# Placing the modulation's column sums in the wait of the norm behind the MLP, and multiplying the first two input panels together

## The chip, the cores and the metric

The kernel runs on 1 core of one Trainium2 chip, in one launch. The metric is the device time in microseconds (us) from the first to the last instruction with what lies around them; lower is better. The core has five engines that run in parallel, each through its own instructions in order: TensorE (PE, matrix products into PSUM, eight banks of 128x512 float32), VectorE (DVE), ScalarE (ACT), GpSimd (POOL) and SyncE (SP, which only issues DMAs here). They wait for each other on semaphores.

## The reference

Two transformer-like blocks over x of 512 tokens by 1024 features, all float32. The first is an RWKV-7 branch and a short convolution, gated and merged, then cross attention to a memory, then an MLP. The second is a gated window attention and a spatial gating unit under an adaptive norm. The change lies at the seam of the two:

```python
# end of the first block
hm = rms_norm(x, norm_mlp)
x = x + jnp.square(jax.nn.relu(hm @ w_up)) @ w_down        # w_up 1024x4096, w_down 4096x1024
x = rms_norm(x, norm_final)
# start of the second block
ada = silu(c) @ w_ada + b_ada                              # c: 1024, w_ada: 1024x3072
shift, scale, gate = jnp.split(ada, 3)
h = _rms(x, g_pre) * (1.0 + scale) + shift
proj = h @ w_in                                            # split into q, k, v, z_a, u_b, v_b, z_b, gate logits
...
x = x + gate * _rms(y, g_post)                             # the last line; x is the residual
```

## The kernel before, in words

**Layout.** Activations lie feature-major: a tile is 128 features by 512 tokens, and a tensor of 1024 features is 8 tiles (KT = 8). xT is the residual. Every large product is cut into panels of 128 output features. A panel's weights, 128x1024 float32, come in one DMA of 512 KB on SP's queue into one of three slots (w_raw, W = 3); ACT rounds them to w_hi, DVE writes the rest w_raw - w_hi to w_lo, and the operand is split into opX_hi and opX_lo the same way. A panel is then 8 steps of 3 matmuls (w_hi by hi, w_hi by lo, w_lo by hi), 24 matmuls of 128x512, summed into bank 0 or bank 1 by turns.

**What sets the order.** The order is written out by hand. SEGMENTS names 210 panels in sequence: ..., up3 (8 panels), down3 (8), qkv (7), ub (4), vb (4), za, zb, gates2 and so on. Each engine has a program that walks the same sequence with the class Panels: begin(i) waits on PE for the panel's w_lo and for its bank to be emptied, step(i, k) is one of the 8 steps (on ACT and DVE the steps K_HIGH = 5 and K_LOW = 6 make w_hi and w_lo of panel i + 2), and end(i) is what ACT, DVE or POOL do with the result. multiply() issues begin and all steps of one panel without its end, leave() the end, to(name) whole panels up to a segment. What stands between these calls is placed there by hand. SP waits for panel i - 3 to be multiplied before it issues panel i's DMA into the same slot.

**The seam.** ada_sum holds silu(c) times w_ada, summed over the 8 row tiles by DVE during down0 and down1: 128 partial sums for each of 3072 columns. Summing these over the partitions needs PE: 24 matmuls ("columns"), each with 128 columns of ada_sum as weights and one column of a constant as the moving operand (L361, out 128x1). In float32 each shows as two records in the profile, so 48. Before, all 24 stand between up3 and down3 and write bank 6; DVE then makes adac (24 columns: shift, scale, gate), gain2, gain3 and gate2 in four small instructions. During down3 ACT squares each new residual tile twice (plain, and times norm_final) and POOL adds the squares to acc and acc2. Behind down3's last panel, two norms follow each other without a tile-wide step between: PE sums acc over the partitions (token_sums, 4 columns, 8 records, into bank 7) and acc2 (bank 6), DVE and ACT form 1/rms as a column, DVE widens it (token_wide), and PE turns it into a row over tokens (token_spread, 4 transposes of 128x128, into bank 5). Then DVE and ACT make opA_hi and opA_lo of the 8 tiles in turn: scale(k) on DVE, the high part on ACT, the low part on DVE. The first panel of qkv starts with tile 0 and waits at each step (operand_low).

**Behind the first panel.** During qkv's first panel DVE widens the first norm's column (r1c to r1, rstd_first), PE spreads it into bank 6 behind that panel, and DVE scales the residual in eight instructions: xT times norm_final times bank 6. These stand on DVE ahead of the copy that empties bank 1 of the first panel. The scaled residual is read only at the very end (last_add).

Of the kernel before, what the change touches and what calls it, by code (L numbers as in the profile page):

```python
# [10 lines left out]
D = 1024  # L11
# [108 lines left out]
class Panels:  # L120
# [18 lines left out]
    def leave(self):  # L139
        self.end(self.i)  # L140
        self.i, self.k = self.i + 1, 0

    def to(self, name):
# [5 lines left out]
def build(nc, x_in, mem_in, panels, ada_w, vec_in, mat_in, win_in, lora_in, pos_in, sink_in, ws_in,  # L149
# [111 lines left out]
    def mat(name):  # L261
        a, w = MAT[name]
        return mats[:, a:a + w]
# [33 lines left out]
    def left_after(i):  # L297
# [49 lines left out]
        sem("angle_step"), sem("sine"), sem("rotated"), sem("rope_cosine"), sem("rope_sine"), sem("rope_made"))  # L347
    silu_half = sem("silu_sigmoid")

# [7 lines left out]
    def tensor_program():  # L357
        pe = nc.tensor

        def mm(o, lhsT, rhs, start=True, stop=True):  # L360
            return pe.matmul(o, lhsT, rhs, start=start, stop=stop, skip_group_check=True)  # L361
# [307 lines left out]
        p.leave()  # L669
        p.to("down3")  # L670
        pe.wait_ge(ada_step, KT)
        for c in range(24):
            ins = mm(bank[6][:, c:c + 1], ada_sum[:, c * NP:(c + 1) * NP], mat("mean")[:, 0:1])
        ins.then_inc(ada_mm, 1)
        p.to("qkv")
        pe.wait_ge(summed, 2 + 3 * KT)
        token_sums(acc, bank[7])
        pe.wait_ge(summed2, KT)
        token_sums(acc2, bank[6])
        token_spread(rstd, bank[5], 1)  # L680
        p.multiply()
        token_spread(r1, bank[6], 2)
        p.leave()
        p.to("za")
# [406 lines left out]
    def gpsimd_program():  # L1091
# [145 lines left out]
        gp.memset(acc[:, :], 0.0).then_inc(cleared, 1)  # L1237
        p.to(None)
        for n, k in enumerate((0, 2, 4)):
            gp.wait_ge(sv_step, 12 + k + 1)  # L1240
            tt(xT[:, k, :], xT[:, k, :], P[:, k, :], ALU.add).then_inc(last_add, 1)

    def vector_program():
        ve = nc.vector

        def tt(o, a, b, op):
            return ve.tensor_tensor(o, a, b, op)  # L1247
# [39 lines left out]
        def end(i):  # L1287
# [61 lines left out]
            elif name[:4] == "down":  # L1349
                tt(xT[:, m, :], ps, xT[:, m, :], ALU.add).then_inc(left[j], 1)  # L1350
            elif name == "qkv":
                ve.tensor_copy(P[:, m, :], ps).then_inc(left[j], 1)
            elif name in ("za", "zb"):
                ve.wait_ge(silu_half, (0 if name == "za" else 4) + m + 1)
                tt(P[:, (ZA if name == "za" else ZB) + m, :], ps, tmp[j][:, :], ALU.mult).then_inc(left[j], 1)
            elif name == "out2":
                ve.wait_ge(squared, 5 * KT + m + 1)
                ts(P[:, m, :], ps, gate2[:, m:m + 1], ALU.mult).then_inc(left[j], 1)
# [196 lines left out]
        for h in range(XH):  # L1555
# [13 lines left out]
        p.leave()  # L1569
        p.to("down3")  # L1570
        ve.wait_ge(ada_mm, 1)
        stt(adac, bank[6][:, 0:24], float(D), vecs[:, COL["b_ada"]:COL["b_ada"] + 24], ALU.mult,
            ALU.add).then_inc(ada_cols, 1)
        ve.wait_ge(ada_cols, 1)
        stt(gain2, adac[:, 8:16], 1.0, vecs[:, COL["g_pre"]:COL["g_pre"] + 8], ALU.add, ALU.mult).then_inc(ada_cols, 1)
        ve.wait_ge(ada_cols, 2)
        tt(gain3, gain2, vecs[:, COL["norm_final"]:COL["norm_final"] + 8], ALU.mult).then_inc(ada_cols, 1)
        tt(gate2, adac[:, 16:24], vecs[:, COL["g_post"]:COL["g_post"] + 8], ALU.mult).then_inc(ada_cols, 1)
        p.to("qkv")

# [14 lines left out]
        token_reciprocal(head_cols, 1)  # L1595
        token_wide(rc, rstd)
        ve.wait_ge(tok_spread, 1)
        ve.wait_ge(ada_cols, 4)
# [9 lines left out]
        for k in range(KT):  # L1608
# [3 lines left out]
            if k + 2 < KT:  # L1612
                scale(k + 2)
        p.multiply()
        token_wide(r1c, r1)
        ve.wait_ge(tok_spread, 2)
        for k in range(KT):
            stt(xT[:, k, :], xT[:, k, :], vec("norm_final", k), bank[6][:, :], ALU.mult, ALU.mult)
        p.leave()
        p.to("ub")  # L1620
# [227 lines left out]
```

## Time and profile before

| what | value |
|---|---|
| time, median of 3 runs | 1542.4 us (1537.39 to 1544.82) |
| the profiled execution's own time | 1547.85 us |
| its span, first to last instruction | 1546.5 us |
| mean granted TensorE clock | 0.97 of full |
| PE busy | 1454.3 us, 94% of the span |
| DVE, ACT, POOL busy | 788.1, 484.9, 171.2 us |
| HBM read | 130.86 MB, 86 GB/s over the span |

The profiled execution took 1.35 us more than its span; that is launch and end. It is 5.45 us above the median and above all three timed runs, so differences are worked out inside the trace and then taken from the median. PE waits for little; its clock is granted at one of two levels, shown as 1.00 (2.4 GHz) or 0.50 (1.2 GHz). A window's value between the two is a mix. Matmuls overlap, so the distance between two starts is what one costs, not its length: 128x512 shows 0.40 us of length at full clock and starts every 0.23 us.

### The profile page before, as it was taken

The numbers are of one execution on the slowest core, as the hardware profiler recorded it, in microseconds if no ns is written. First come the engines' busy times: TensorE is split into PE (matmuls) and PEld (weight loads), VectorE is DVE, ScalarE is ACT, GpSimd is POOL, SyncE is SP. The second block draws the span as 40 slices with busy tenths as digits, with TensorE's granted clock in tenths as the row PEclk, the third lists the DMA queues.
The fourth block names the chain that finished last, engine by engine and source line by source line (L and its number), as shares of the span: only waits on it lengthen the run. The fifth ranks groups of instructions, "written<-read, shape, count | busy, mean of one in ns | idle before, by whom it ended". The sixth has DMA issues, their size and how long they took to land.

```text
span 1546.5 us, 21133 instructions
## 1 busy us (share of the span) xinstructions
PE 1454.3 (94%) x9170; PEld 1138.3 (74%) x9170; DVE 788.1 (51%) x1069; ACT 484.9 (31%) x716; POOL 171.2 (11%) x155
## 2 busy tenths in 40 slices
PE   4999999999998999998999999999989999998995
PEld 3677686877766878876877787888867777777784
DVE  5364363645538654534464655535345344565544
ACT  4321222314134343224431222212232332663331
POOL 1120110202011220000200000000130011003122
PEclk9999899999998999999999999999889999999997
DMA  4110111112014224420244434322222223221221
GB/s 152 60 56 29 41 43 42 56 43 69 29 59 146 96 82 151 134 71 15 95 169 171 167 105 163 96 95 94 70 68 73 91 83 99 77 69 55 95 93 72
DMA packets 37579, 134.34 MB, mean 87 GB/s; under 512 B 4045, under 2 KB 5709, under 8 KB 36462
## 3 DMA queue, kind: packets, MB, share of 16 engines
q1 hardware_dynamic: 31392, 112.21, 21.7%
q0 software_dynamic: 1440, 13.63, 2.4%
q10 hardware_dynamic: 4654, 7.13, 1.4%
q8 instruction: 73, 1.20, 0.3%
q14 instruction: 20, 0.16, 0.0%
HBM read 130.86 MB, written 2.10 MB: 86 GB/s over the span
## 4 chain that ended last, share of the span: by engine, by line
PE 37%; issue 14%; DVE 6%; DMA 3%; ACT 3%; POOL 1%; POOLq 0%; DVEq 0%
PE bank L361 36%; DMA w_raw<-panels 3%; DVE w_lo L1247 1%; ACT w_hi L773 1%; POOL acc L1095 1%; PE bank L364 1%; ACT scores L773 1%; ACT L773 0%; DVE ada_sum L1255 0%; DVE xT L1247 0%; DVE tmp L1255 0%; DVE P L1247 0%; DVE tmp L1247 0%; ACT exp L773 0%; DVE xT L1255 0%
## 5 line engine op out<-in xcount | busy, mean ns | idle before, releaser
L361 PE MATMUL bank<-opA_hi,w_hi 128*128 128x512 f32 x1104 | 466.1, 422 | 39.2 <-DVE opA_lo L1255 18.3
L1247 DVE TENSOR_TENSOR w_lo<-w_raw,w_hi 128x1024 fp32r<-128x1024 f32 x210 | 261.4, 1246 | 387.7 <-ACT w_hi L773 387.7
L361 PE MATMUL bank<-opA_lo,w_hi 128*128 128x512 f32 x1104 | 443.0, 401 | 0.0
L361 PE MATMUL bank<-opA_hi,w_lo 128*128 128x512 f32 x1104 | 442.5, 401 | 0.0
L773 ACT ACTIVATE w_hi<-w_raw 128x1024 fp32r<-128x1024 f32 x210 | 221.8, 1057 | 433.3 <-DMA w_raw<-panels 430.9
L361 PEld LDWEIGHTS bank<-opA_hi,w_hi 128*128 128x128 f32 x1104 | 211.3, 191 | 105.1 <-issue 41.6
L361 PEld LDWEIGHTS bank<-opA_hi,w_lo 128*128 128x128 f32 x1104 | 211.7, 192 | 51.8
L361 PEld LDWEIGHTS bank<-opA_lo,w_hi 128*128 128x128 f32 x1104 | 212.2, 192 | 45.3 <-issue 2.7
L361 PE MATMUL bank<-opB_hi,w_hi 128*128 128x512 f32 x448 | 180.0, 402 | 6.9 <-DVE xT L1247 4.3
L361 PE MATMUL bank<-opB_lo,w_hi 128*128 128x512 f32 x448 | 178.4, 398 | 0.0
L361 PE MATMUL bank<-opB_hi,w_lo 128*128 128x512 f32 x448 | 178.4, 398 | 0.0
L361 PEld LDWEIGHTS bank<-opB_hi,w_hi 128*128 128x128 f32 x448 | 85.1, 190 | 29.5 <-issue 5.8
L361 PEld LDWEIGHTS bank<-opB_hi,w_lo 128*128 128x128 f32 x448 | 85.0, 190 | 20.8
L361 PEld LDWEIGHTS bank<-opB_lo,w_hi 128*128 128x128 f32 x448 | 85.2, 190 | 20.5 <-issue 0.2
L1095 POOL TENSOR_TENSOR acc<-acc,sq 128x512 f32<-128x512 f32 x32 | 43.0, 1344 | 374.3 <-issue 266.8
L773 ACT ACTIVATE opB_hi<-tmp 128x512 fp32r<-128x512 f32 x44 | 27.8, 632 | 106.8 <-DVE tmp L1255 62.9
L773 ACT ACT_TABLE_LOAD x40 | 51.3, 1283 | 6.4 <-DMA w_raw<-panels 5.7
L361 PE MATMUL bank<-mem_hi,w_hi 128*128 128x256 f32 x128 | 36.7, 287 | 3.3 <-DVE kvT L1247 3.3
L1247 DVE TENSOR_TENSOR xT<-bank,xT 128x512 f32<-128x512 f32 x48 | 32.9, 685 | 9.7 <-PE bank L361 9.7
L361 PE MATMUL bank<-mem_lo,w_hi 128*128 128x256 f32 x128 | 36.2, 283 | 0.0
L361 PE MATMUL bank<-mem_hi,w_lo 128*128 128x256 f32 x128 | 36.2, 282 | 0.0
L773 ACT ACTIVATE UV<-bank 64x64 f32<-64x64 f32 (+1 forms) x40 | 11.6, 291 | 72.0 <-PE bank L361 72.0
(272 smaller groups left out, 1451.2 us busy)
## 6 DMA issues: line engine op xcount, KB each, us to landing
w_raw<-panels SPq DMA_DIRECT2D x210, 512.0 KB, 3.5
ada_w<-ada POOLq DMA_DIRECT2D x8, 1536.0 KB, 7.6
xT<-x ACTq DMA_DIRECT2D x1, 2048.0 KB, 11.2
out<-xT SPq DMA_DIRECT2D x8, 256.0 KB, 2.1
xT<-x POOLq DMA_DIRECT2D x2, 512.0 KB, 10.0
xT<-x ACTq DMA_DIRECT2D x2, 512.0 KB, 12.1
memT<-mem ACTq DMA_DIRECT2D x1, 1024.0 KB, 13.5
mats<-mat ACTq DMA_DIRECT2D x1, 672.0 KB, 7.6
```

What stands on the lines that cost most here:

```text
L361: return pe.matmul(o, lhsT, rhs, start=start, stop=stop, skip_group_check=True)
L364: return pe.transpose(o, i, mat("ident"))
L773: return ac.activation(o, i, f, **kw)
L1095: return gp.tensor_tensor(o, a, b, op)
L1247: return ve.tensor_tensor(o, a, b, op)
```

## The change

The 24 column matmuls leave their place between up3 and down3. They are issued in three groups of 8 in the wait behind down3: part 1 (scale) into bank 3 ahead of the token sums, part 0 (shift) into bank 2 behind them and ahead of the spread, part 2 (gate) into bank 4 behind the spread. DVE's small instructions follow them, in groups of the same order. The first two panels of qkv are multiplied by the new method pair(), which issues step k of the one (bank 1) and step k of the other (bank 0) before step k + 1. The spread of the first norm's row moves behind both. DVE's eight instructions on the residual move to the four ends of the ub panels, two each, and POOL waits for all eight (x3_made) ahead of its last additions.

```diff
--- before.py
+++ after.py
@@ -139,6 +139,15 @@
     def leave(self):
         self.end(self.i)
         self.i, self.k = self.i + 1, 0
+
+    def pair(self):
+        self.begin(self.i)
+        self.begin(self.i + 1)
+        for k in range(KT):
+            self.step(self.i, k)
+            self.step(self.i + 1, k)
+        self.leave()
+        self.leave()
 
     def to(self, name):
         assert self.k == 0
@@ -345,7 +354,7 @@
         sem("token_spread"), sem("x4_scaled"))
     angle_step, trig_done, rot_mm, rope_pool, rope_sin, rope_done = (
         sem("angle_step"), sem("sine"), sem("rotated"), sem("rope_cosine"), sem("rope_sine"), sem("rope_made"))
-    silu_half = sem("silu_sigmoid")
+    silu_half, x3_made = sem("silu_sigmoid"), sem("x3_made")
 
     assert N_PANELS == panels.shape[0], (N_PANELS, panels.shape)
     sink_done, bn_step, ws_mm, ws_done, vn_v, vn_g, uz_done, sv_mm, sv_step = (
@@ -667,20 +676,24 @@
         pe.wait_ge(summed, 2 + 2 * KT)
         mean(acc, S)
         p.leave()
-        p.to("down3")
+        p.to("qkv")
+
+        def ada_columns(part):
+            for c in range(KT * part, KT * (part + 1)):
+                ins = mm(bank[2 + part][:, c:c + 1], ada_sum[:, c * NP:(c + 1) * NP], mat("mean")[:, 0:1])
+            ins.then_inc(ada_mm, 1)
+
         pe.wait_ge(ada_step, KT)
-        for c in range(24):
-            ins = mm(bank[6][:, c:c + 1], ada_sum[:, c * NP:(c + 1) * NP], mat("mean")[:, 0:1])
-        ins.then_inc(ada_mm, 1)
-        p.to("qkv")
+        ada_columns(1)
         pe.wait_ge(summed, 2 + 3 * KT)
         token_sums(acc, bank[7])
         pe.wait_ge(summed2, KT)
         token_sums(acc2, bank[6])
+        ada_columns(0)
         token_spread(rstd, bank[5], 1)
-        p.multiply()
+        ada_columns(2)
+        p.pair()
         token_spread(r1, bank[6], 2)
-        p.leave()
         p.to("za")
 
         def rotate(n, t):
@@ -1236,6 +1249,7 @@
         gp.wait_ge(weigh_mm, 2 * XH + 4)
         gp.memset(acc[:, :], 0.0).then_inc(cleared, 1)
         p.to(None)
+        gp.wait_ge(x3_made, KT)
         for n, k in enumerate((0, 2, 4)):
             gp.wait_ge(sv_step, 12 + k + 1)
             tt(xT[:, k, :], xT[:, k, :], P[:, k, :], ALU.add).then_inc(last_add, 1)
@@ -1350,6 +1364,10 @@
                 tt(xT[:, m, :], ps, xT[:, m, :], ALU.add).then_inc(left[j], 1)
             elif name == "qkv":
                 ve.tensor_copy(P[:, m, :], ps).then_inc(left[j], 1)
+            elif name == "ub":
+                ve.wait_ge(tok_spread, 2)
+                for k in range(2 * m, 2 * m + 2):
+                    stt(xT[:, k, :], xT[:, k, :], vec("norm_final", k), bank[6][:, :], ALU.mult, ALU.mult).then_inc(x3_made, 1)
             elif name in ("za", "zb"):
                 ve.wait_ge(silu_half, (0 if name == "za" else 4) + m + 1)
                 tt(P[:, (ZA if name == "za" else ZB) + m, :], ps, tmp[j][:, :], ALU.mult).then_inc(left[j], 1)
@@ -1567,16 +1585,19 @@
         p.multiply()
         inv_root(rstd[:, :], bank[7][:, :], 4)
         p.leave()
-        p.to("down3")
-        ve.wait_ge(ada_mm, 1)
-        stt(adac, bank[6][:, 0:24], float(D), vecs[:, COL["b_ada"]:COL["b_ada"] + 24], ALU.mult,
-            ALU.add).then_inc(ada_cols, 1)
+        p.to("qkv")
+
+        def ada_columns(part, n):
+            c = slice(KT * part, KT * (part + 1))
+            ve.wait_ge(ada_mm, n)
+            stt(adac[:, c], bank[2 + part][:, c], float(D), vecs[:, COL["b_ada"] + KT * part:COL["b_ada"] + KT * (part + 1)],
+                ALU.mult, ALU.add).then_inc(ada_cols, 1)
+
+        ada_columns(1, 1)
         ve.wait_ge(ada_cols, 1)
         stt(gain2, adac[:, 8:16], 1.0, vecs[:, COL["g_pre"]:COL["g_pre"] + 8], ALU.add, ALU.mult).then_inc(ada_cols, 1)
         ve.wait_ge(ada_cols, 2)
         tt(gain3, gain2, vecs[:, COL["norm_final"]:COL["norm_final"] + 8], ALU.mult).then_inc(ada_cols, 1)
-        tt(gate2, adac[:, 16:24], vecs[:, COL["g_post"]:COL["g_post"] + 8], ALU.mult).then_inc(ada_cols, 1)
-        p.to("qkv")
 
         def token_reciprocal(v, n):
             ve.wait_ge(tok_root, n)
@@ -1594,6 +1615,7 @@
         stt(rc, r1c, EPS, bank[6][:, 0:4], ALU.mult, ALU.add).then_inc(tok_var, 1)
         token_reciprocal(head_cols, 1)
         token_wide(rc, rstd)
+        ada_columns(0, 2)
         ve.wait_ge(tok_spread, 1)
         ve.wait_ge(ada_cols, 4)
 
@@ -1611,12 +1633,10 @@
                 ALU.subtract).then_inc(op_lo, 1)
             if k + 2 < KT:
                 scale(k + 2)
-        p.multiply()
+        ada_columns(2, 3)
+        ve.wait_ge(ada_cols, 5)
+        tt(gate2, adac[:, 16:24], vecs[:, COL["g_post"]:COL["g_post"] + 8], ALU.mult).then_inc(ada_cols, 1)
         token_wide(r1c, r1)
-        ve.wait_ge(tok_spread, 2)
-        for k in range(KT):
-            stt(xT[:, k, :], xT[:, k, :], vec("norm_final", k), bank[6][:, :], ALU.mult, ALU.mult)
-        p.leave()
         p.to("ub")
 
         TURN, MAGIC = 2 * np.pi, 1.5 * 2 ** 23
```

ACT's and SP's instructions stand in the same order before and after. Three places show the rest. In all of them opA and opB are the operands, w_hi2 is slot 2 of the high weights, and the number behind an underscore is a buffer's own. Line numbers of the change are 9 to 23 higher than before for the same helper.

The first place is PE behind the last matmul of down3, before:

```order
L361 MATMUL bank0<-opB_hi_52,w_lo1_58 128x512
L361 MATMUL bank7<-mats_74,acc_71 128x1 [waits squares_summed]
L361 MATMUL bank7<-mats_74,acc_71 128x1 x3
L361 MATMUL bank6<-mats_74,acc2_72 128x1 [waits squares2_summed]
L361 MATMUL bank6<-mats_74,acc2_72 128x1 x3
L364 MATMUL bank5<-mats_74,rstd_64 128x128 [waits token_wide]
L364 MATMUL bank5<-mats_74,rstd_64 128x128 x3
```

and in the change:

```order
L370 MATMUL bank0<-opB_hi_52,w_lo1_58 128x512
L370 MATMUL bank3<-mats_74,ada_sum_127 128x1 [waits ada_step]
L370 MATMUL bank3<-mats_74,ada_sum_127 128x1 x7
L370 MATMUL bank7<-mats_74,acc_71 128x1 [waits squares_summed]
L370 MATMUL bank7<-mats_74,acc_71 128x1 x3
L370 MATMUL bank6<-mats_74,acc2_72 128x1 [waits squares2_summed]
L370 MATMUL bank6<-mats_74,acc2_72 128x1 x3
L370 MATMUL bank2<-mats_74,ada_sum_127 128x1 x8
L373 MATMUL bank5<-mats_74,rstd_64 128x128 [waits token_wide]
L373 MATMUL bank5<-mats_74,rstd_64 128x128 x3
L370 MATMUL bank4<-mats_74,ada_sum_127 128x1 x8
```

acc and acc2 are the sums of squares, rstd the widened column of the norm. The three groups of ada_sum matmuls now stand ahead of the token sums, between these and the spread, and behind the spread; the 24 that stood between up3 and down3 are gone from there.

The second place is PE at the end of qkv's first panel and the start of the second, before:

```order
L361 MATMUL bank1<-opA_hi_50,w_hi2_62 128x512 [waits operand_low]
L361 MATMUL bank1<-opA_lo_51,w_hi2_62 128x512
L361 MATMUL bank1<-opA_hi_50,w_lo2_59 128x512
L364 MATMUL bank6<-mats_74,rstd_first_73 128x128 [waits token_wide]
L364 MATMUL bank6<-mats_74,rstd_first_73 128x128 x3
L361 MATMUL bank0<-opA_hi_50,w_hi0_60 128x512 [waits bank0_left,panel_low_made]
L361 MATMUL bank0<-opA_lo_51,w_hi0_60 128x512
L361 MATMUL bank0<-opA_hi_50,w_lo0_57 128x512
```

and in the change, PE from the first step of the pair:

```order
L370 MATMUL bank1<-opA_hi_50,w_hi2_62 128x512 [waits bank0_left,panel_low_made,operand_low,bank1_left]
L370 MATMUL bank1<-opA_lo_51,w_hi2_62 128x512
L370 MATMUL bank1<-opA_hi_50,w_lo2_59 128x512
L370 MATMUL bank0<-opA_hi_50,w_hi0_60 128x512
L370 MATMUL bank0<-opA_lo_51,w_hi0_60 128x512
L370 MATMUL bank0<-opA_hi_50,w_lo0_57 128x512
L370 MATMUL bank1<-opA_hi_50,w_hi2_62 128x512 [waits operand_low]
```

and PE from the end of its last step:

```order
L370 MATMUL bank0<-opA_lo_51,w_hi0_60 128x512
L370 MATMUL bank0<-opA_hi_50,w_lo0_57 128x512
L373 MATMUL bank6<-mats_74,rstd_first_73 128x128 [waits token_wide]
L373 MATMUL bank6<-mats_74,rstd_first_73 128x128 x3
L370 MATMUL bank1<-opA_hi_50,w_hi1_61 128x512 [waits bank1_left,panel_low_made]
```

Bank 1 and slot 2 belong to the first panel of qkv, bank 0 and slot 0 to the second, slot 1 to the third. Six matmuls stand behind each wait for an operand tile where three stood, and the four transposes of rstd_first stand ahead of the third panel where they stood ahead of the second.

The third place is DVE from the last operand tile on, before:

```order
L1255 SCALAR_TENSOR_TENSOR opA_lo_51<-tmp1_68,cols_76,opA_hi_50 128x512 [waits operand_high]
L1247 TENSOR_TENSOR w_lo1_58<-w_raw1_55,w_hi1_61 128x1024 [waits panel_high_made]
L1587 COPY rstd_first_73<-cols_76 128x512
L1255 SCALAR_TENSOR_TENSOR xT_49<-xT_49,vecs_75,bank6 128x512 [waits token_spread]
L1255 SCALAR_TENSOR_TENSOR xT_49<-xT_49,vecs_75,bank6 128x512 x7
L1352 COPY P_63<-bank1 128x512 [waits panel_multiplied]
L1247 TENSOR_TENSOR w_lo2_59<-w_raw2_56,w_hi2_62 128x1024 [waits panel_high_made]
L1352 COPY P_63<-bank0 128x512 [waits panel_multiplied]
```

and in the change:

```order
L1269 SCALAR_TENSOR_TENSOR opA_lo_51<-tmp1_68,cols_76,opA_hi_50 128x512 [waits operand_high]
L1269 SCALAR_TENSOR_TENSOR cols_76<-bank4,vecs_75 128x8 [waits ada_multiplied]
L1261 TENSOR_TENSOR cols_76<-cols_76,vecs_75 128x8 [waits ada_columns]
L1608 COPY rstd_first_73<-cols_76 128x512
L1261 TENSOR_TENSOR w_lo1_58<-w_raw1_55,w_hi1_61 128x1024 [waits panel_high_made]
L1366 COPY P_63<-bank1 128x512 [waits panel_multiplied]
L1261 TENSOR_TENSOR w_lo2_59<-w_raw2_56,w_hi2_62 128x1024 [waits panel_high_made]
L1366 COPY P_63<-bank0 128x512 [waits panel_multiplied]
```

Further on in the change, DVE at the ends of the first two ub panels:

```order
L1266 TENSOR_SCALAR sq1_70<-sq1_70 128x512 [waits angle_step]
L1265 TENSOR_SCALAR sq1_70<-sq1_70 128x512 [waits angle_step]
L1269 SCALAR_TENSOR_TENSOR xT_49<-xT_49,vecs_75,bank6 128x512 [waits token_spread]
L1269 SCALAR_TENSOR_TENSOR xT_49<-xT_49,vecs_75,bank6 128x512
L1261 TENSOR_TENSOR w_lo0_57<-w_raw0_54,w_hi0_60 128x1024 [waits panel_high_made]
L1269 SCALAR_TENSOR_TENSOR xT_49<-xT_49,vecs_75,bank6 128x512 [waits token_spread]
```

cols holds adac and the gains, P the results of qkv, sq the sine's argument. The eight instructions on xT stood ahead of the copy that empties bank 1; now two small ones stand ahead of w_lo1, and the residual is scaled by twos ahead of each w_lo in ub. The w_lo2 of qkv's fourth panel stands between the copies of the first two panels in both.

## Rows read from the trace of the kernel before

**Rows 1.** the profile page, part 1: busy time and share of the span.
```profile
PE 1454.3 (94%) x9170; PEld 1138.3 (74%) x9170; DVE 788.1 (51%) x1069; ACT 484.9 (31%) x716; POOL 171.2 (11%) x155
```

**Rows 2.** windows over every engine, from up3 to the norm; columns in the first row.
```profile
core 0: us, PE busy (x) PEld busy (x) DVE busy (x) ACT busy (x) POOL busy (x), PEclk, DMA share, GB/s
1090.76:1091.76 1.00, 1.00 (x11) 1.00 (x9) 0.96 (x3) 0.03 (x1) 0.00 (x0) 1.00 0.00 0
1094.20:1095.20 1.00, 1.00 (x6) 1.00 (x6) 0.00 (x0) 0.77 (x1) 0.00 (x0) 0.50 0.00 0
1103.47:1145.87 42.40, 42.40 (x182) 33.81 (x180) 12.83 (x14) 16.15 (x21) 17.83 (x14) 1.00 0.26 87
1151.00:1153.50 2.50, 1.12 (x4) 0.72 (x4) 0.94 (x5) 0.21 (x1) 0.00 (x0) 0.52 0.00 0
```

**Rows 3.** timeline of PE, up3 to down3: start, length, engine, line, operation [idle before it].
```profile
1090.76 8.12 PE L361 MATMUL bank<-mats,ada_sum 128*128 128x1 f32 x48
1098.74 0.77 PE L361 MATMUL bank<-opB_hi,w_hi 128*128 128x512 f32 x1
...
1103.47 0.40 PE L361 MATMUL bank<-opB_hi,w_lo 128*128 128x512 f32 x1
```

**Rows 4.** timeline of all engines, the wait of the norm behind down3.
```profile
1145.90 0.69 DVE L1247 TENSOR_TENSOR xT<-bank,xT 128x512 f32<-128x512 f32 x1
...
1148.56 1.26 POOL L1095 TENSOR_TENSOR acc<-acc,tmp 128x512 f32<-128x512 f32 x1
...
1149.87 1.05 PE L361 MATMUL bank<-mats,acc 128*128 128x1 f32 x8 [0.17 <-POOL acc L1095]
...
1152.31 1.12 PE L364 MATMUL bank<-mats,rstd 128*128 128x128 f32 x4 [1.39 <-DVE rstd L1587]
...
1155.00 0.75 DVE L1255 SCALAR_TENSOR_TENSOR opA_lo<-tmp,cols,opA_hi 128x512 fp32r<-128x512 f32 x1
...
1155.90 0.76 PE L361 MATMUL bank<-opA_hi,w_hi 128*128 128x512 f32 x1 [2.47 <-DVE opA_lo L1255]
```

**Rows 5.** timeline of PE, the first two panels of qkv and the start of the third.
```profile
1161.17 0.48 PE L361 MATMUL bank<-opA_hi,w_lo 128*128 128x512 f32 x1
...
1167.13 0.66 PE L364 MATMUL bank<-mats,rstd_first 128*128 128x128 f32 x4 [0.80 <-DVE rstd_first L1587]
1167.54 0.48 PE L361 MATMUL bank<-opA_hi,w_hi 128*128 128x512 f32 x1
...
1173.93 0.47 PE L361 MATMUL bank<-opA_hi,w_hi 128*128 128x512 f32 x1 [0.55 <-DVE P L1352]
```

**Rows 6.** timeline of DVE, the same stretch.
```profile
1157.90 0.75 DVE L1255 SCALAR_TENSOR_TENSOR opA_lo<-tmp,cols,opA_hi 128x512 fp32r<-128x512 f32 x1
...
1159.34 0.75 DVE L1255 SCALAR_TENSOR_TENSOR opA_lo<-tmp,cols,opA_hi 128x512 fp32r<-128x512 f32 x1
...
1167.82 5.36 DVE L1255 SCALAR_TENSOR_TENSOR xT<-xT,vecs,bank 128x512 f32<-128x512 f32 x8 [0.75 <-PE bank L364]
```

**Rows 7.** the tile w_raw, whole span (duration ns min/median/max), then its first 12 us.
```profile
L773 ACT ACTIVATE w_hi<-w_raw x210: 1039/1060/1064, 8.8 to 1514.7; 128x1024 fp32r<-128x1024 f32 x105
...
DMA to landing us min/median/max: 3.3/3.5/10.0
...
DMA to landing us min/median/max: 4.0/7.1/10.0
```

**Rows 8.** timeline of PE, a third restart at half clock, in ub.
```profile
1216.63 0.76 PE L361 MATMUL bank<-opA_hi,w_hi 128*128 128x512 f32 x1 [3.27 <-ACT P L773]
...
1222.74 0.42 PE L361 MATMUL bank<-opA_hi,w_lo 128*128 128x512 f32 x1
```

**Rows 9.** timeline of DVE, between the panels of ub.
```profile
1217.46 1.23 DVE L1247 TENSOR_TENSOR w_lo<-w_raw,w_hi 128x1024 fp32r<-128x1024 f32 x1 [3.55 <-ACT w_hi L773]
...
1229.99 1.22 DVE L1247 TENSOR_TENSOR w_lo<-w_raw,w_hi 128x1024 fp32r<-128x1024 f32 x1 [9.87 <-ACT w_hi L773]
```

## The prediction, made before the changed kernel ran

> **What bounds the kernel now.** I read the page first: PE is busy for 94% of the span, no other engine for more than 51% [rows 1]. So each microsecond in which PE does something other than full-width matmuls at full clock is on the path, unless another engine is late at that place. Then the windows: from 1103.47 to 1145.87 us PE is busy throughout, at clock 1.00, and starts 182 matmuls in 42.40 us, 0.233 us each [rows 2]; a panel of 24 costs 5.6 us. Then PE's timeline at the three places that the change touches: the columns between up3 and down3 [rows 3], the wait of the norm [rows 4], and the first panels of qkv [rows 5].
>
> **The columns between up3 and down3.** The 48 records start at 1090.76, down3 starts at 1098.74: 7.98 us [rows 3]. PE is in order and everything that down3 reads is on time: the last opB_lo of up3 is needed only by the eighth step of down3's first panel, 7 x 0.70 = 4.9 us in, so nothing is late when the columns go. The clock falls inside them: one window holds 11 records at 1.00, a later one 6 at 0.50 [rows 2], so a record costs about 0.1 us or 0.17 us. Behind them the first 11 matmuls of down3 run at half clock: 1098.74 to 1103.47 is 4.73 us, 0.43 each, where 11 x 0.233 = 2.56 would do [rows 3]. That is another 2.17 us, and without the columns PE has no reason to slow there: what precedes is dense. First terms: -7.98 and -2.17.
>
> **Group one, ahead of the token sums.** down3's last result is taken up by DVE at 1145.90, POOL finishes acc2 at 1148.56 + 1.26 = 1149.82, and the first token sums wait for acc, ready when acc2's addition starts, about 1148.6 [rows 4]. The 16 records cost 1.6 us at full clock and 2.7 at half; 2.7 us are free. Cost 0. DVE's three small instructions behind them lie in DVE's own wait.
>
> **Group two, ahead of the spread.** The second token sums start at 1149.87, and their 8 records are issued by about 1150.8; the spread started at 1152.31 once DVE had widened rstd [rows 4]. Into this gap of 1.5 us go 16 records. At full clock they take 1.6 and cost about 0.1. But from 1151.0 to 1153.5 the clock is 0.52 [rows 2], so I take 2.7 us: the spread starts near 1153.5, 1.2 us later. Bounds: 0 (all at full clock) to 1.9 (token sums slowed too).
>
> **Group three, behind the spread.** The first operand tile is ready when opA_lo is written, 1155.00 + 0.75 = 1155.75, and PE started at 1155.90 [rows 4], 3.6 us after the spread's start. The spread shows 1.12 us with the drain of its last result, some 0.8 to issue, and 16 records at half clock take 2.7: 3.5 us. They just fit. So the pair starts at 1155.90 + 1.2 = 1157.1. Bounds of this part: 0 to 1.0, if a record costs 0.2 and its last result has to drain.
>
> **The pair.** Before, PE got a new operand tile every 1.44 us from DVE [rows 6], and used it for 3 matmuls: 1.29 us at half clock, 0.70 at full. It waited, and half clock cost it nothing there. Then 0.80 us for rstd_first, a spread of 0.41 (1167.13 to 1167.54), 24 matmuls, and 0.55 us for DVE's copy out of the bank, which stood behind eight instructions on xT (5.36 us) [rows 5, 6]. The third panel started at 1173.93, 18.03 us after the first. Now each tile feeds 6 matmuls: 2.6 us at half clock, 1.40 at full, so PE stays behind DVE at half clock and level with it later, where it has fallen back enough not to wait. After restarts this trace shows 11 matmuls at half clock [rows 3], 12 (1155.90 to 1161.17) [rows 5], and 14 (1216.63 to 1222.74) [rows 8]. With 12: 12 x 0.43 + 36 x 0.233 = 13.6 us, from 1157.1 to 1170.7. The spread of rstd_first, whose column is long ready, adds 0.45: third panel at 1171.2, against 1173.93. Third term: -2.7. Bounds: with 11 or 14 half-clock matmuls -2.9 to -2.3; with the bounds of the two groups -4.1 to -0.6.
>
> The Trainium skill, page "TensorE: Matmul & The Clock Gate", section "Back-to-back issue gap", gives N/2.4 + 2.5 ns, here 216 ns, per full-clock matmul; the rows show 233. By an estimate from the page the pair would end 36 x 0.017 = 0.6 us earlier and the sum would be -13.5; the rows decide.
>
> **What is late next.** With the pair, panels one and two finish 0.7 us apart, and their slots come free only then. Before, panel one freed its slot at about 1166.3, ahead of the spread [rows 5], a whole panel before the second. The fourth panel's DMA now starts at about 1170.2 (panel one's last matmul at 1169.8 plus the 0.4 that a result takes), lands 3.5 us later, ACT needs 1.06 [rows 7], DVE 1.23 [rows 9], and the copy of bank 1 stands behind that w_lo on DVE, 0.7: 1176.8. PE wants to start that panel at 1171.2 + 5.6 = 1176.8. No slack, no cost; I count 0. The copy of bank 0's predecessor, panel one, is done at 1171.0, inside the spread. Bounds: 0 to 3.6 us, if the transfer takes 7.1 as the second of three in a row did at the start [rows 7].
>
> **The residual's scaling.** Eight instructions of 0.67 us leave DVE where PE waited for it (that 0.55 us is in the third term) and go by twos to the ends of ub. DVE idles 3.55 us ahead of the w_lo of ub's fourth panel and 9.87 us ahead of that of vb's second [rows 9]; 1.34 us fit. The sine's chain that makes PE wait 3.27 us in ub [rows 8] stands ahead of them. Cost 0, bound 1.3 if one of the w_lo were due. POOL's new wait (x3_made) is met long before its turn, which comes at the program's end. The SP queue keeps its order.
>
> **Sum.** -7.98 - 2.17 - 2.7 = -12.9 us. On the profiled execution that is 1547.85 - 12.9 = 1535.0; the median of before is 5.45 lower, so 1542.4 - 12.9 = 1529.5 us. What the measurement can tell from no change is about 0.5%, 7.7 us: above 1534.7 counts as the same.
>
> **Rivals.**
> 1. The fourth panel comes late. Two panel DMAs are issued 0.7 us apart; the kernel's start shows landings of 4.0, 7.1 and 10.0 us for three issued together [rows 7]. If the first of the two is slowed to the 7.1, PE waits 3.6 us: 1533.1. Against: at the start other loads share the engines, and even there the first landed at 4.0. Chance 0.10.
> 2. The columns' 8 us covered something, and down3 waits for it instead. Speaking for it: DVE and ACT were idle for most of those 8 us, so their lateness would not be seen. Against: from 1103.47 on PE never waits in down3 with the same pitch of DMA, ACT and DVE. If all of it came back, only the third term would remain: 1539.7. Chance 0.04.
> 3. The pair stays at half clock. All 48 matmuls at 0.43 take 20.6 us, 36 x 0.197 = 7.1 more: 1536.6. The Trainium skill, the same page, section "A second HAM failure mode: psum-queue depth-cycling", tells of a kernel that went through PSUM banks by turns, whose clock oscillated because PE idled briefly between groups. Here banks 0 and 1 alternate every three matmuls. Against it: the rows of PE's start pitch show no gap at any change of bank in down3, at clock 1.00 [rows 2]. Chance 0.04.
> 4. Slower than before. The same mechanism at the same place, but PE does not get its clock back: the pair, with gaps wherever it catches up with DVE, and the five qkv panels behind it. Each matmul costs 0.197 more at half clock. The gain is gone after 12.9 / 0.197 = 65 such matmuls beyond the 12, that is 29 beyond the pair, and the time is measurably slower after another 39. Over all five panels (120): -12.9 + 7.1 + 23.6 = +17.8, 1560. Against: all three restarts recovered within 14 matmuls [rows 3, 5, 8]. Chance 0.03.
> 5. The change doesn't do what it says, because groups two and three land on the path. At the upper bounds the third term is -0.6: 1531.7, inside the forecast's own range.
>
> **Numbers.** Forecast 0.79, rivals one to four 0.10, 0.04, 0.04, 0.03. The forecast's own range is 1528 to 1532 from the bounds; the runs of before scatter by 5 below and 2 above their median, which widens it. The 8-in-10 range is 1524 to 1536. Faster by over 0.5%: the forecast and most of rival one, 0.87. Same: rivals two and three and the tail of one, 0.10. Slower: 0.03.
>
> **What would show it.** Right: down3 starts 0.2 us behind up3's last matmul at clock 1.00; 16 records fill 1.6 us of the norm's wait; the spread starts 0 to 2 us later against the last down3 matmul; the pair shows 11 to 15 starts at 0.43 and then 0.233; the third panel starts 25.3 us behind the end of down3 (28.06 before). Wrong: a wait of PE in down3's first two panels, an idle time ahead of the fourth qkv panel with DVE w_lo or P as releaser, or half clock beyond the pair. The forecast fails if the columns' time returns elsewhere or if the clock's pattern at the other waits, which shift by 10 us, comes out worse by more than 5 us.

## The result, and the profile after

The changed kernel takes 1534.25 us, median of 11 runs (1525.3 to 1536.96), against 1541.3 us for the kernel before in 11 runs (1537.39 to 1550.36): a ratio of 0.994, 95% interval 0.9923 to 0.9957. The medians are 7.05 us apart; the means (1542.0 and 1532.2) are 9.8 apart, with an interval of 6.5 to 13.1, and the ratio of 0.994 would be 9 us. 1534.25 lies inside the predicted range of 1524 to 1536, 4.75 us above the predicted 1529.5 and 0.45 us under the 1534.7 from which the prediction would have counted it as no change.

The page's first part answers to [rows 1]:

```profile
span 1523.7 us, 21136 instructions
...
PE 1440.4 (95%) x9170; PEld 1131.4 (74%) x9170; DVE 789.2 (52%) x1071; ACT 484.6 (32%) x716; POOL 171.6 (11%) x155
```

PE is still what bounds the kernel, and its busy time is 13.9 us less. The profiled execution took 1525.3 us, the lowest of its 11 runs, and that of before (1547.85) was above ten of the 11 that it is compared with here. The two profiled executions are therefore 22.6 us apart where the medians are 7 apart, and the difference has to be taken stage by stage. Timeline of PE in the changed kernel: the seam of up3 and down3 (opA gives way to opB), the end of down3, the norm's wait, the first panels of qkv. Columns: start us, length us, engine, line, operation, tiles, count, idle before and releaser.

```profile
1084.65 0.40 PE L370 MATMUL bank<-opA_hi,w_lo 128*128 128x512 f32 x1
1084.88 0.40 PE L370 MATMUL bank<-opB_hi,w_hi 128*128 128x512 f32 x1
...
1129.45 0.40 PE L370 MATMUL bank<-opB_hi,w_lo 128*128 128x512 f32 x1
1129.68 1.84 PE L370 MATMUL bank<-mats,ada_sum 128*128 128x1 f32 x16
...
1132.64 1.05 PE L370 MATMUL bank<-mats,acc 128*128 128x1 f32 x8 [1.12 <-POOL acc L1108]
1133.86 1.05 PE L370 MATMUL bank<-mats,acc 128*128 128x1 f32 x8 [0.17 <-POOL acc L1108]
1134.77 3.39 PE L370 MATMUL bank<-mats,ada_sum 128*128 128x1 f32 x16
1138.02 1.09 PE L373 MATMUL bank<-mats,rstd 128*128 128x128 f32 x4
1138.91 3.41 PE L370 MATMUL bank<-mats,ada_sum 128*128 128x1 f32 x16
1142.18 0.77 PE L370 MATMUL bank<-opA_hi,w_hi 128*128 128x512 f32 x1
1142.75 0.63 PE L370 MATMUL bank<-opA_lo,w_hi 128*128 128x512 f32 x1
...
1144.89 0.54 PE L370 MATMUL bank<-opA_hi,w_hi 128*128 128x512 f32 x1
1145.27 0.40 PE L370 MATMUL bank<-opA_lo,w_hi 128*128 128x512 f32 x1
...
1154.60 0.39 PE L370 MATMUL bank<-opA_hi,w_lo 128*128 128x512 f32 x1
1154.83 0.60 PE L373 MATMUL bank<-mats,rstd_first 128*128 128x128 f32 x4
1155.18 0.48 PE L370 MATMUL bank<-opA_hi,w_hi 128*128 128x512 f32 x1
...
1160.90 0.47 PE L370 MATMUL bank<-opA_hi,w_hi 128*128 128x512 f32 x1
```

Read it against [rows 3 to 5]. down3 starts 0.23 us behind up3; the 7.98 us and the half-clock matmuls behind them are gone. The 192 matmuls of down3 take 1129.68 - 1084.88 = 44.80 us, 0.233 each. The norm's wait, from the place where a next matmul could have started (1129.68) to the first of qkv (1142.18), is 12.50 us; before it was 1155.90 - 1145.70 = 10.20. The pair with its spread takes 1155.18 - 1142.18 = 13.00 us instead of 18.03. The third panel starts 25.50 us behind that place, before 28.23 (the prediction counted both from the last matmul's end, 0.17 us later: 25.3 and 28.06). The fourth panel follows with next to no wait, at 1160.90. Together: -7.98 - 2.16 + 2.30 - 5.03 = -12.87 us at the seam of this pair of traces.

The rest is no work of the change. The spans of the two traces differ by 22.8 us: 5.9 lie ahead of up3's last matmul, where nothing was changed (1090.53 against 1084.65), 12.87 at the seam, and 4.1 behind the start of the third qkv panel (372.6 and 368.5 us to the end). That last stretch is 371.1 us in a second profile of the kernel before and 371.5 in a second one of the changed kernel (e6 and e3 below), so nothing of the gain is seen to be lost behind the seam. Windows of the first stage (rw, 360 panel matmuls and the small ones between them) and of ub, first of the kernel before, then of the changed one; the column in tenths of full behind POOL is the granted clock:

```profile
14.89:187.72 172.83, 162.27 (x1304) 115.02 (x1305) 87.30 (x135) 46.77 (x74) 23.16 (x22) 0.93 0.14 45
1202.00:1230.70 28.70, 25.43 (x98) 20.04 (x97) 10.49 (x16) 8.89 (x10) 0.00 (x0) 0.88 0.27 85
```

```profile
14.90:181.35 166.45, 155.81 (x1305) 111.61 (x1305) 87.13 (x135) 46.80 (x74) 23.47 (x22) 0.98 0.13 47
1183.37:1209.29 25.92, 22.64 (x98) 17.96 (x97) 14.35 (x22) 8.89 (x10) 0.00 (x0) 1.00 0.27 96
```

In rw both kernels issue the same instructions, and it is 6.4 us shorter at clock 0.98 than at 0.93. In ub the changed kernel does more on DVE (22 instructions, not 16) and is 2.8 us shorter, at 1.00 against 0.88. Where PE waits a few microseconds the clock sometimes falls and sometimes doesn't, whatever the kernel: e3, the same changed kernel, shows ub at 28.8 us again, and in e4, whose ub is that of the kernel before, the clock stays at 1.00.

### The profile page after: what moved, and what is told of

It is laid out like the page before. It is cut to its first block, busy times and chain, and to the rows that moved or that the text cites. A ratio compares the mean times of both kernels' runs of the same rounds, so it can differ in the third digit from the quotient of the medians.

```text
span 1523.7 us, 21136 instructions
## 1 busy us (share of the span) xinstructions
PE 1440.4 (95%) x9170; PEld 1131.4 (74%) x9170; DVE 789.2 (52%) x1071; ACT 484.6 (32%) x716; POOL 171.6 (11%) x155
## 4 chain that ended last, share of the span: by engine, by line
PE 39%; issue 13%; DVE 5%; ACT 3%; DMA 3%; POOL 1%; POOLq 0%; DVEq 0%
PE bank L370 38%; DMA w_raw<-panels 3%; POOL acc L1108 1%; DVE w_lo L1261 1%; ACT w_hi L786 1%; ACT scores L786 1%; PE bank L373 1%; ACT L786 1%; DVE ada_sum L1269 0%; DVE xT L1261 0%; DVE P L1261 0%; DVE tmp L1261 0%; ACT exp L786 0%; DVE v_norm L1261 0%; DVE scores L1261 0%
## 5 line engine op out<-in xcount | busy, mean ns | idle before, releaser
L370 PE MATMUL bank<-opA_hi,w_hi 128*128 128x512 f32 x1104 | 460.4, 417 | 34.4 <-DVE opA_lo L1269 14.9
L786 ACT ACTIVATE P<-tmp,vecs 128x512 f32<-128x512 f32 x16 | 11.6, 724 | 70.0 <-DVE tmp L1261 70.0
```

The lines of the kernel that those rows point to most:

```text
L786: return ac.activation(o, i, f, **kw)
```

## The experiments

Two theories stood against each other at the start. The first (A in the expectations) is the prediction's sum: the columns give back what they took on PE, the norm's wait grows little, and the pair saves some 4 us by itself. The second (B) is that the 5 us by which the median fell short came back elsewhere, as half clock at other waits; beside it stands the idea that the columns had covered something in down3. A third (C) came with the traces: that the sum was taken from a profile in which the seam happened to be dear. For each kernel the seam was measured from PE's starts as above:

| kernel | gap | tail | wait | pair | sum |
|---|---|---|---|---|---|
| before, first profile | 7.98 | 2.16 | 10.20 | 18.03 | 38.4 |
| e6, before again | 5.28 | 1.63 | 10.38 | 18.03 | 35.3 |
| e5, residual only | 5.85 | 2.64 | 11.56 | 17.31 | 37.4 |
| e4, columns twice | 15.43 | 1.71 | 10.42 | 18.03 | 45.6 |
| e2, pair only | 6.00 | 2.49 | 11.51 | 13.69 | 33.7 |
| e1, columns only | 0 | 0 | 14.04 | 17.44 | 31.5 |
| changed kernel | 0 | 0 | 12.50 | 13.00 | 25.5 |
| e3, changed again | 0 | 0 | 13.47 | 13.61 | 27.1 |
| e7, two groups early | 0 | 0 | 11.52 | 12.95 | 24.5 |
| e8, filled wait | 0 | 0 | 12.68 | 12.63 | 25.3 |

(us. Gap: between up3 and down3. Tail: what down3's start at half clock costs over 0.233 us per matmul. Wait: the norm's. Pair: start of qkv to start of its third panel.)

**e1: the columns alone.** The placement of the columns of the changed kernel, with qkv's panels and the residual as before.

```diff
-        p.to("down3")
         pe.wait_ge(ada_step, KT)
-        for c in range(24):
-        ...
+        ada_columns(1)
         ... (token sums)
+        ada_columns(0)
         token_spread(rstd, bank[5], 1)
+        ada_columns(2)
         p.multiply()
```

> The kernel before with one part of the change: the 24 columns in three groups of 8 in the wait of the norm. No pair, residual scaled where it was. Theory A (the sum of terms holds): 10.15 us go between up3 and down3 (7.98 of columns, 2.17 of half clock behind them); the groups put the first operand tile back by 2.3 us, as the trace of the change shows (12.33 us from the end of down3 to the first matmul of qkv, 10.03 before), and with one panel at a time PE follows DVE, so all 2.3 are paid: -7.9 us, ratio 0.9949. Theory B (part of what goes at the columns returns elsewhere as half clock at other waits, which shows in the timed runs but not inside the seam): about -4 us, ratio 0.997. In the trace both: down3 starts 0.2 us behind up3.

Measured: 1535.76 us, median of 12 runs; ratio 0.9963 (0.9943 to 0.9983). The profile of e1, PE in the norm's wait:

```profile
1129.23 1.84 PE L370 MATMUL bank<-mats,ada_sum 128*128 128x1 f32 x16
...
1132.26 3.57 PE L370 MATMUL bank<-mats,acc 128*128 128x1 f32 x16 [1.19 <-POOL acc L1109]
1135.69 3.55 PE L370 MATMUL bank<-mats,ada_sum 128*128 128x1 f32 x16
1139.11 1.09 PE L373 MATMUL bank<-mats,rstd 128*128 128x128 f32 x4
1139.99 3.41 PE L370 MATMUL bank<-mats,ada_sum 128*128 128x1 f32 x16
1143.27 0.77 PE L370 MATMUL bank<-opA_hi,w_hi 128*128 128x512 f32 x1
```

The columns alone are worth about two thirds of the gain, and nothing of down3 comes late: the idea that their 8 us had covered something falls. The times alone don't decide between A and B: by means it is 5.9 us (2.9 to 8.9). The seam is 6.9 us shorter than in the first profile of before and 3.8 shorter than in e6, under A's 7.9 both times: the wait grew by 3.8 and 3.7 us (3.2 against the mean of the five unchanged waits of the table), not by 2.3. Here the clock is low from the token sums on: their 16 records take 3.43 us. What goes in behind them at half clock costs 3.4 us a group, 0.214 a record.

**e2: the pair alone,** with the spread behind it and the residual's scaling in ub, the columns where they were.

```diff
         token_spread(rstd, bank[5], 1)
-        p.multiply()
+        p.pair()
         token_spread(r1, bank[6], 2)
-        p.leave()
         ... (the residual's eight instructions to the ends of ub, as in e5)
```

> The kernel before with the other part: the first two panels of qkv as a pair, the spread of the first norm behind both, the residual scaled at the ends of ub. The columns stay between up3 and down3. Theory A: the pair starts 10.03 us behind down3 as before, takes 12 x 0.43 + 36 x 0.233 = 13.6 us, third panel 24.1 us behind down3's end where it was 28.06: -4.0 us, ratio 0.9974 (-5 with 7 half-clock matmuls as in the trace of the change). Theory B says nothing else here. If the alternation of banks cost something it would show as a start pitch over 0.233.

Measured: 1538.99 us, median of 12; ratio 0.9999 (0.9977 to 1.0021). The trace and the times part here. In the trace the first two panels take 13.69 us instead of 18.03, 4.3 us less, and nothing behind them is late; the times show no gain. A run's time at half clock is worked out from its span s and its mean granted clock c, as 2(1 - c)s. The 12 runs of e2 had 80.0 us of it on average, those of before 73.3 (difference 6.7, interval -0.7 to 14.2). Over the 88 runs of the six kernels that ran more than once, a straight line with a level for each kernel through the span against the time at half clock gives 0.37 us per microsecond (interval 0.34 to 0.39) and leaves a scatter of 1.2 us of the 3.9. By that line e2 is 3.8 us shorter than before at the same time at half clock (interval 2.9 to 4.6). So the trace and the line show the pair's gain, and the times by themselves don't: by means e2 is 0.7 us shorter (from 3.5 shorter to 2.2 longer). The line also takes out any half clock that the edit itself brings or saves; that e2's runs drew more of it by chance, and not because of the edit, isn't shown.

**e3: the changed kernel again,** on the chip of e1 and e2.

> The change itself once more, beside its parts on the same chip. Theory A: -12.9 us, ratio 0.9916. Theory B: as it was measured, -7 to -9 us, ratio 0.994 to 0.9955. Sum of parts by A: -7.9 - 4.0 = -11.9; the two parts should add up within 1 to 2 us either way, since the pair hides part of the 2.3 us.

Measured: 1531.65 us, median of 6; ratio 0.9936 (0.9913 to 0.996). The two measurements of the change agree. The interval holds theory A's 0.9916 as well as B's range, so the time of e3 decides between them no more than that of e1. B's 5 us would need some 13 us more at half clock, an estimate from the line's 0.37. The 17 runs of the changed kernel had 70.4 us of it, those of before 73.3 (difference -2.9, interval -8.1 to 2.3), of which some 6 us less are the seam's own in the profiles. So a few microseconds more elsewhere aren't excluded, 13 are. By the line of e2, e1's and e2's differences, 5.9 and 3.8, add up to 9.7; the change shows 8.7 (interval 7.9 to 9.4). At equal clock the parts add up within a microsecond. By means they don't show it: 5.9 and 0.7 against 10.1, each with some 3 us of uncertainty.

**e4: the columns twice,** the 24 written into bank 6 a second time in the old place.

```diff
-        for c in range(24):
+        for c in [*range(24), *range(24)]:
```

> The kernel before with the 24 columns issued twice at their old place, into the same bank. Theory A: the second 24 are all at half clock, 48 records of 0.17 to 0.18 us: +8.2 to +8.7 us, ratio 1.0055; the half-clock stretch behind them stays as it was. If columns at that place are partly hidden, the ratio is under 1.003.

Measured: 1551.0 us, median of 6; ratio 1.0063 (1.0039 to 1.0087). By means, 24 more columns cost 8.8 us (5.3 to 12.3). In its trace the gap is 15.43 us, 9.15 more than the mean of the four single ones (7.98, 5.28, 5.85, 6.00: 6.28), and the tail of down3 is no longer than elsewhere:

```profile
1088.10 15.57 PE L361 MATMUL bank<-mats,ada_sum 128*128 128x1 f32 x96
1103.53 0.77 PE L361 MATMUL bank<-opB_hi,w_hi 128*128 128x512 f32 x1
1104.10 0.63 PE L361 MATMUL bank<-opB_lo,w_hi 128*128 128x512 f32 x1
...
1106.66 0.61 PE L361 MATMUL bank<-opB_lo,w_hi 128*128 128x512 f32 x1
1107.09 0.42 PE L361 MATMUL bank<-opB_hi,w_lo 128*128 128x512 f32 x1
```

Columns between two dense segments are on the path in full, and a second set adds no second tail. Here the first 48 records take 5.28 us at clock 1.00 and the second 48, from 1093.37 on, 10.16 us at 0.50, 0.21 a record. That is more than the 0.17 to 0.18 expected; the size was read from the same short window as the prediction's.

**e5 and e6: the residual's scaling alone, and the kernel before once more.** One run each, for the seam of unchanged code.

```diff
         token_wide(r1c, r1)
-        ve.wait_ge(tok_spread, 2)
-        for k in range(KT):
-            stt(xT[:, k, :], ...)
         ...
+            elif name == "ub":
+                ve.wait_ge(tok_spread, 2)
+                for k in range(2 * m, 2 * m + 2):
+                    stt(xT[:, k, :], ...).then_inc(x3_made, 1)
```

> The kernel before with only the residual's eight instructions moved to the ends of ub. The copy that empties bank 1 is then on time, two panels take 17.45 to 17.5 instead of 18.03 us, and ub is as before: 28.7 or 25.9 us by the clock. A third draw of the unchanged columns and the unchanged wait, as theory C has them.

> The kernel before once more, for a second profile. Theory A (the seam's terms are fixed sizes): 7.98 us of columns, 2.16 of half clock behind them, 10.20 from down3's last issue to qkv, 18.03 for two panels. Theory C (they depend on where the clock falls, and the profile of before was one draw): columns and what is behind them 8.5 to 10.2, the wait 10.2 to 11.5, two panels 18.0.

Measured: e5 1543.31 us and e6 1538.04 us, beside 1543.04, median of 11, for before. e6 is the same program as before, and its columns take:

```profile
1085.18 5.41 PE L361 MATMUL bank<-mats,ada_sum 128*128 128x1 f32 x48
...
1139.85 1.05 PE L361 MATMUL bank<-mats,acc 128*128 128x1 f32 x8 [2.80 <-POOL acc L1095]
...
1143.68 1.11 PE L364 MATMUL bank<-mats,rstd 128*128 128x128 f32 x4 [1.39 <-DVE rstd L1587]
1147.26 0.77 PE L361 MATMUL bank<-opA_hi,w_hi 128*128 128x512 f32 x1 [2.47 <-DVE opA_lo L1255]
```

5.28 us of gap, not 7.98, and 3.1 us less over the seam. This is the run that bears out the third theory: the 48 records are the same, and the clock falls 2.3 us into them (before, at 1093.08) or just behind them (e6, at 1090.62, 0.16 us after down3's start). Columns and tail, 6.91 us together, are even under the 8.5 to 10.2 that theory C gave. e5 shows that without DVE's eight instructions the third panel starts 0.72 us earlier against the first (17.31 us, not 18.03): the 0.55 us that PE waited for the copy of the first panel [rows 5], and a little more (17.45 to 17.5 was expected).

**e7: two groups ahead of the token sums,** where PE waits for POOL with nothing to do, and the last group in halves ahead of the spread and behind it.

```diff
         ada_columns(1)
+        ada_columns(0)
         pe.wait_ge(summed, 2 + 3 * KT)
         ... (token sums)
-        ada_columns(0)
+        ada_some(2, 0, 4)
         token_spread(rstd, bank[5], 1)
-        ada_columns(2)
+        ada_some(2, 4, 8).then_inc(ada_mm, 1)
```

> The change with parts 1 and 0 (16 columns, 32 records) both ahead of the token sums, and part 2 in two halves of 4 columns ahead of and behind the spread. Theory A and C: 32 records at full clock are 3.3 us where POOL's acc2 is ready 4.0 us in, so the sums' end stays; 8 records are 0.8 to 1.4 us in a gap of 1.5; the wait becomes 10.3 to 11.7 us instead of 12.5 to 13.5, two panels 13.0 to 14.0 since PE starts earlier and has a few more matmuls at half clock. Against the change -1.5 us, against before -11 to -12: ratio 0.992 to 0.993. Rival: the columns ahead of the sums make the clock fall earlier and the sums are late; then the wait is 13 us or more and nothing is gained.

Measured: 1530.23 us, median of 6; ratio 0.9919 (0.9893 to 0.9946), the lowest of all. Its PE:

```profile
1132.13 3.63 PE L370 MATMUL bank<-mats,ada_sum 128*128 128x1 f32 x32
1135.62 2.90 PE L370 MATMUL bank<-mats,acc 128*128 128x1 f32 x16
1138.38 1.85 PE L370 MATMUL bank<-mats,ada_sum 128*128 128x1 f32 x8
1140.09 1.09 PE L373 MATMUL bank<-mats,rstd 128*128 128x128 f32 x4
1140.97 1.71 PE L370 MATMUL bank<-mats,ada_sum 128*128 128x1 f32 x8
1143.65 0.77 PE L370 MATMUL bank<-opA_hi,w_hi 128*128 128x512 f32 x1 [0.97 <-DVE opA_lo L1275]
```

The first 32 records run at full clock, 0.109 us each (3.49 us). The half group ahead of the spread takes 1.71 us, over the 0.8 to 1.4 expected. PE waits for DVE again ahead of qkv (0.97 us): the half group behind the spread is off the path. The seam is 1.0 us shorter than in the first profile of the change and 2.6 shorter than in the second. Between it and the changed kernel the times don't decide: by means 1530.1 against 1531.7, with some 3 us of uncertainty.

**e8: the wait filled.** e7 with six full-width matmuls that nobody reads, to keep PE busy in the wait.

```diff
         ada_some(2, 0, 4)
+        filler(2)
         token_spread(rstd, bank[5], 1)
         ada_some(2, 4, 8).then_inc(ada_mm, 1)
+        filler(4)
```

> The same with full-width matmuls whose result nobody reads in the two gaps of the wait, 2 ahead of the spread and 4 behind the last columns. If the clock can be held by them: no matmul of the pair at half clock, two panels 12.0 us (DVE's pace of 1.44 us a tile). If it falls all the same: the fillers cost 0.43 each, the wait is 13 to 14 us, and the pair recovers sooner than with 7 to 10 matmuls.

Measured in one run: 1532.53 us. PE's rows from the columns to qkv's first starts:

```profile
1138.98 2.36 PE L370 MATMUL bank<-mats,acc 128*128 128x1 f32 x16
...
1142.91 1.20 PE L370 MATMUL bank<-opB_hi 128*128 128x512 f32 x2
1143.91 1.06 PE L373 MATMUL bank<-mats,rstd 128*128 128x128 f32 x4
1144.76 1.71 PE L370 MATMUL bank<-mats,ada_sum 128*128 128x1 f32 x8
1146.32 2.05 PE L370 MATMUL bank<-opB_hi 128*128 128x512 f32 x4
1148.18 0.63 PE L370 MATMUL bank<-opA_hi,w_hi 128*128 128x512 f32 x1
```

The fillers run at half clock themselves (1.86 us for four). Against e7 the wait is 1.16 us longer and the pair 0.32 us shorter: 6 matmuls at half clock instead of 7. The clock had fallen at 1140.30, ahead of the first filler. Filling shows no gain here, but this is one profile, and the unchanged wait itself varies between profiles by 1.36 us (10.20 to 11.56). Whether fillers ahead of the fall would hold the clock was not tried.

## Why the prediction was right, and which terms were mis-sized

**The mechanism.** Most of what the prediction said would show is in the traces: down3 0.23 us behind up3, no wait in it, the first group free in POOL's wait, the third panel 2.73 us closer to the end of down3 (forecast -2.7), no wait to speak of ahead of the fourth. One sign didn't come: 11 to 15 starts at half clock in the pair, where the first profile has 7. e1, e2 and e3 show the two halves each by itself and together.

**"First terms: -7.98 and -2.17".** This is the term that was too large. Both numbers are right for the one profile that they came from, and that profile was the dearest of four with the columns in the old place: gap and tail are 10.14, 6.91, 8.49 and 8.49 us, 8.5 on average, not 10.15. The prediction subtracted them from the median of the runs, though the profiled execution stood 5.45 us above it. A place where the clock may fall has a range of prices, and one profile shows one of them. With 8.5 the sum is 11.2 us.

**"So I take 2.7 us: the spread starts near 1153.5, 1.2 us later", and group three at 0.** The two groups cost 2.30 us together. In the trace of the change a group takes 1138.02 - 1134.77 = 3.25 us, almost all of it at half clock, 0.203 a record, and wholly at half clock 0.214 (e1); the prediction had 0.17, from a window of one microsecond that held six records [rows 2], too short to tell five from six. So the spread came 1.72 us later against the second token sums (inside the bounds of 0 to 1.9), and from the spread to the first matmul of qkv it is 4.16 us instead of 3.59 (0.57, inside 0 to 1.0): the third group did not "just fit". In e3, where the clock fell 4.4 us behind down3's last start and not 5.5, the second token sums were slow too (1.72 us, not 0.91) and the wait was 13.47.

**The pair.** 12 matmuls at half clock were counted, 7 and 10 were seen in the two profiles of the change, so that the pair took 13.00 and 13.61 us instead of 14.05. The later start may have a part in it: in the profiles of before, of the change, of e7 and of e8 the granted clock is back at 15.9, 15.8, 14.7 and 15.3 us behind down3's last start, though qkv begins between 10.4 and 12.9 us behind it, so that more of the low stretch falls into the wait and less into the pair. It is no rule: in e3 the clock is back at 18.1 and in e1 at 20.0. The two errors in these terms, +1.1 and -1.05, cancel in the first profile, and this is why the -2.7 came out. That was luck: against e6, the second profile of the change (e3) gives 13.47 - 10.38 + 13.61 - 18.03 = -1.3. The mean of the two is -2.0, and against the mean wait of the five profiles whose wait is unchanged (10.81) it is -2.5.

**The sum as measured.** Seams of before 38.4 and 35.3, of the change 25.5 and 27.1: 10.5 us between the means, 8.5 for gap and tail and 2.0 for the third term (11.0 with the -2.5). The times of all runs, 46 of before and 17 of the change, differ by 9.8 us between the means (7.6 to 12.0). The forecast -12.9 is outside that, -10.5 and -11.0 are inside: the mechanism was right, and the forecast landed in its range with its first terms 1.6 us and its third 0.2 to 0.7 us too large. The predicted 1529.5 was 3.1 us below the median of the 17, 1532.6.

**The rivals.** The fourth panel is late by next to nothing: the two transfers land 3.5 and 4.5 us after their issue, and PE starts 0.27 us behind the third panel's last start, where 0.23 is the pitch. ACT, then DVE, at that panel in the changed kernel:

```profile
1157.84 1.06 ACT L786 ACTIVATE w_hi<-w_raw 128x1024 fp32r<-128x1024 f32 x1 [6.67 <-DMA w_raw<-panels]
1159.50 1.06 ACT L786 ACTIVATE w_hi<-w_raw 128x1024 fp32r<-128x1024 f32 x1 [0.60 <-DMA w_raw<-panels]
```

```profile
1158.92 1.23 DVE L1261 TENSOR_TENSOR w_lo<-w_raw,w_hi 128x1024 fp32r<-128x1024 f32 x1 [3.90 <-ACT w_hi L786]
1160.07 0.68 DVE L1366 COPY P<-bank 128x512 f32<-128x512 f32 x1
```

The w_lo is ready at 1160.15, and the bank is empty at 1160.75, for a start at 1160.90: no slack, as was said, and a cost of 0.04 us, with 0.08 more in the matmul behind (0.31 us to the next start). Rival two fell with e1. Rival three, the pair at half clock, fell in each of the five profiles with the pair (6 to 11 matmuls at half clock). The window over the rest of it in the changed kernel, 1.00 behind POOL's column, has 41 records in 9.30 us:

```profile
1145.30:1154.60 9.30, 9.30 (x41) 7.49 (x40) 7.45 (x13) 3.70 (x5) 0.00 (x0) 1.00 0.00 0
```

The Trainium skill, page "TensorE: Matmul & The Clock Gate", section "A second HAM failure mode: psum-queue depth-cycling", ties the oscillating clock to PE idling between groups. Here banks change every three matmuls without an idle time, and the clock doesn't oscillate; that agrees with the rule, which then doesn't apply. The slower case needed the clock to stay low behind the pair, and no profile shows that.

**The range.** It was set from the bounds plus the scatter of before. What could have corrected the centre was the same scatter, read the other way: that the profile's own time is above all three of its companions is a hint that its clock rows are dear ones. It is no more than that: e2's profile lies 1.5 us under its median, and its gap and tail are still 8.49 us.

## What to carry to other kernels

Narrow matmuls between two dense segments are on the path in full and in each of the five profiles that have them there the clock fell in them or just behind; put them into a wait that PE has anyway, first into the part in which its clock is still high, and count those behind at the half-clock rate (0.214 us a record here, 0.109 at full). When a term rests on where the clock fell in one profile, look at how that execution stands among its runs and take the term from the middle of what several profiles show. When the operand tiles are made more slowly than PE uses them at a restart (1.44 us a tile here, against 0.70 to 1.29 us for its three matmuls), feeding two panels from each tile turns PE's wait into work.

## What the runs showed of the hardware that was not expected

In these traces DVE's small instructions with both sources in SBUF last until POOL's running tensor_tensor ends. Timeline of DVE, then of POOL, in the changed kernel:

```profile
1131.56 0.17 DVE L1269 SCALAR_TENSOR_TENSOR cols<-bank,vecs 128x8 f32<-128x8 f32 x1 [0.98 <-PE bank L370]
1131.76 0.85 DVE L1269 SCALAR_TENSOR_TENSOR cols<-cols,vecs 128x8 f32<-128x8 f32 x1
1132.64 1.19 DVE L1261 TENSOR_TENSOR cols<-cols,vecs 128x8 f32<-128x8 f32 x1
```

```profile
1131.32 1.26 POOL L1108 TENSOR_TENSOR acc<-acc,sq 128x512 f32<-128x512 f32 x1 [2.93 <-ACT sq L786]
1132.54 1.26 POOL L1108 TENSOR_TENSOR acc<-acc,tmp 128x512 f32<-128x512 f32 x1
```

The two end at 1132.61 and 1133.83, POOL's at 1132.58 and 1133.80. The same instruction takes 0.17 us in e6, where POOL is idle, and 0.92 in e1, where it isn't; the first one, which reads a bank, takes 0.17 us in the midst of POOL's. The 1.7 us lie off the path here: they end 1.1 us ahead of the norm's next instruction on DVE. That these sources are what matters is read from these profiles and was not tried by itself.
